# Moving fill work in a two-layer encoder trunk: the recurrence's evacuation, local attention, sample steps and embedding tiles

## The reference

```
h = x + 0.5 * RMSNorm(SwiGLU_1(RMSNorm(x)))
u = RMSNorm(h); [branch inputs | gate logits] = u @ w_in
four branches on u, each 256 wide:
  A conv module   B HGRN2 gated recurrence   C sliding-window attention   D stick-breaking attention
y_n = o_n @ w_branch[n];  m = sum_n sigmoid(gate_n) * y_n;  mix = m @ w_out
h = h + RMSNorm(mix);  h = h + 0.5 * RMSNorm(SwiGLU_2(RMSNorm(h)))
h = h + RMSNorm((p[i] @ ple_w) * sigmoid(RMSNorm(h) @ ple_gate_w))
```

## Time and profile before

| what | value |
|---|---|
| median of 3 runs | 3288.26 us (3283.48 to 3296.35) |
| profiled execution, its own time | 3279.91 us |
| its span, first to last instruction | 3278.2 us |
| PE busy | 3162.7 us, 96% of the span |
| mean granted clock of PE | 0.982 |
| ACT, DVE, POOL busy | 1079.8, 958.7, 1179.9 us |

### The profile page before, as it was taken

The page is one execution under the profiler, slowest core; times in us unless marked ns, Lnnn a source line. Parts: engine busy times, 40 slices in busy tenths (PEclk is TensorE's granted clock), DMA queues, the critical chain, the costliest instruction groups (busy, mean ns, idle before and its releaser), DMA issues.

```text
span 3278.2 us, 55957 instructions
## 1 busy us (share of the span) xinstructions
PE 3162.7 (96%) x24207; PEld 3049.5 (93%) x24207; DVE 958.7 (29%) x1417; ACT 1079.8 (33%) x1536; POOL 1179.9 (36%) x564
## 2 busy tenths in 40 slices
PE   8999999999999999999999999999999999999998
PEld 8999999996799999999999999989868999999988
DVE  3111024744443311101331110249334433111023
ACT  3233232235433332322433222322454333322222
POOL 6334333331234433333343433323212434333333
PEclk9999999999999999999899999999999999999988
DMA  3222222221122222322122222222211222222211
GB/s 102 83 80 78 83 63 66 78 71 41 45 78 83 58 83 78 88 83 68 58 63 79 83 80 82 65 56 85 62 41 53 82 78 58 83 83 88 81 52 62
DMA packets 455959, 236.31 MB, mean 72 GB/s; under 512 B 18630, under 2 KB 454150, under 8 KB 455814
## 3 DMA queue, kind: packets, MB, share of 16 engines
q1 hardware_dynamic: 445792, 227.05, 23.8%
q10 hardware_dynamic: 10022, 7.15, 0.7%
HBM read 228.53 MB, written 5.63 MB: 71 GB/s over the span
## 4 chain that ended last, share of the span: by engine, by line
PE 89%; DVE 5%; ACT 3%; POOL 1%; issue 1%; ACTq 1%; POOLq 0%; DVEq 0%
PE ps L594 79%; PE ps L626 3%; PE ps L634 1%; PE ps L1538 1%; PE ps L1848 1%; DVE uf L825 1%; PE ps L1556 1%; PE ps L1518 1%; DVE u_lo L819 1%; POOL u_lo L819 1%; ACT u_hi L743 0%; DVE kgate L1135 0%; PE ps L1542 0%; PE ps L1527 0%; DVE att L1153 0%
## 5 line engine op out<-in xcount | busy, mean ns | idle before, releaser
L1988 POOL TENSOR_TENSOR wlo<-wraw,whi 128x1024 fp32r<-128x1024 f32 (+1 forms) x432 | 1042.8, 2418 | 1934.9 <-ACT whi L556 1934.6
L594 PE MATMUL ps<-u_hi,whi 128*128 128x288 f32 x4800 | 1051.4, 300 | 37.5 <-ACT ybr L1714 11.8
L594 PE MATMUL ps<-u_lo,whi 128*128 128x288 f32 x4800 | 1033.8, 296 | 0.0
L594 PE MATMUL ps<-u_hi,wlo 128*128 128x288 f32 x4800 | 1033.3, 296 | 0.0
L594 PEld LDWEIGHTS ps<-u_hi,whi 128*128 128x128 f32 x4800 | 770.2, 189 | 72.6 <-issue 32.9
L594 PEld LDWEIGHTS ps<-u_hi,wlo 128*128 128x128 f32 x4800 | 774.1, 189 | 0.0
L594 PEld LDWEIGHTS ps<-u_lo,whi 128*128 128x128 f32 x4800 | 774.0, 189 | 0.0
L556 ACT ACTIVATE whi<-wraw 128x1024 fp32r<-128x1024 f32 (+1 forms) x432 | 449.3, 1040 | 559.3 <-PE ps L594 332.1
L868 DVE TENSOR_TENSOR sq<-sq,ps 128x576 f32<-128x576 f32 x88 | 66.3, 754 | 900.6 <-PE ps L594 900.6
L594 PE MATMUL ps<-s_hi,whi 128*128 128x288 f32 x1408 | 303.1, 296 | 0.0
L594 PE MATMUL ps<-s_hi,wlo 128*128 128x288 f32 x1408 | 302.7, 296 | 0.0
(11 more groups left out here) (268 smaller groups left out, 2595.5 us busy)
## 6 DMA issues: line engine op xcount, KB each, us to landing
wraw<-in_ffn_up SPq DMA_DIRECT2D x176, 512.0 KB, 3.8
wraw<-in_w_in SPq DMA_DIRECT2D x104, 512.0 KB, 3.8
wraw<-in_ffn_down SPq DMA_DIRECT2D x64, 512.0 KB, 3.7
wraw<-in_ffn_down SPq DMA_DIRECT2D x32, 384.0 KB, 3.4
wraw<-in_w_out SPq DMA_DIRECT2D x16, 512.0 KB, 3.8
wraw<-in_ple_gate_w SPq DMA_DIRECT2D x16, 512.0 KB, 3.8
wraw<-in_w_branch SPq DMA_DIRECT2D x16, 256.0 KB, 2.8
xtok<-in_x_prompt SPq DMA_DIRECT2D x4, 512.0 KB, 6.4
```

The source lines that it names most:

```text
L594: ins = pe.matmul(ps[:, 2 * p + f, 0:HT], wt[:, part, w], x[:, k, HT * f:HT * f + HT], start=start and n == 0 and c == 0, stop=stop and n ...
L1988: pool.tensor_tensor(wlo[:, i % SLOTS, 0:width(i)], wraw[:, i % SLOTS, 0:width(i)], whi[:, i % SLOTS, 0:width(i)], ALU.subtract).then_inc( ...
```

## The change

No product is added or removed. Five things move.

1. **Recurrence.** Two quarters of fill instead of one follow `hg_values` on TensorE, one fewer comes after the factors. On ScalarE, the evacuation and rounding of the unit that ends there, and the table load, go behind the copies and squares of the recurrence.
2. **Local attention.** Its three units of fill go in quarters instead of thirds: eleven steps instead of nine, and the twelfth quarter after the transposes of `pe_sb_tok`. Its evacuation stands behind the four cache stores.
3. **Sample steps.** The two gate-logit units of output tile 0 become kept gates 16 and 17, written to `sg`. `sb_fill` gives steps 16 to 21 two quarters each.
4. **Gates.** For m = 0, TensorE has only the branch unit; the sigmoids are taken from `sg` in place. The hardware loop is written out.
5. **Embedding.** Three tiles stand ahead of the square sums, two among them, one before the root, two after the factors; it was two, three, none and three.

```diff
-            gate_out: 2 * KD, gate_sig: 10,
+            gate_out: 2 * KD + 2, gate_sig: 10,
...
+            N_KEPT = 2 * KD + 2
+            BRANCHES = [U0_PAIR + 2] + [U0_PAIR + 3 * m for m in range(1, KD)]
...
@@ pe_hg, act_hg
                 hg_values(pe)
-                pe_fill(pe, 1)
+                pe_fill(pe, 2)
...
-                act_fill(act, 6)
+                act_fill(act, 5)
...
             def act_hg_norm(act):
-                act.preload_act_table_set(ROOT_SET)
                 for c in range(2):
                     act.wait_ge(hg_out, c + 1 + before(hg_out))
...
                     act.activation(sq[:, c, :], of[:, 2 + c, :], ACT.Square).then_inc(hg_sq, 1)
+                act.preload_act_table_set(ROOT_SET)
+                act_fill(act, 2)
...
-                act_fill(act, 4)
+                act_fill(act, 3)
...
@@ act_gate_part
-                    act.activation(halves(gkeep[:, g, :]), pair(0), ACT.Copy).then_inc(gate_out, 1)
+                    dst = gkeep[:, g, :] if g < 2 * KD else sg[:, g - 2 * KD, :]
+                    act.activation(halves(dst), pair(0), ACT.Copy).then_inc(gate_out, 1)
...
@@ pe_sw (act_sw alike)
-                    pe_gate_part(pe, GATES_CONV, GATES_SW, i, THIRDS)
+                    pe_gate_part(pe, GATES_CONV, GATES_SW, i, QUARTERS)
...
+            def sb_fill(i):
+
+                at = lambda j: min(max(j, 2 * j - 16), 4 * (N_KEPT - GATES_SW))
+                return range(at(i), at(i + 1))
...
@@ pe_sb (act_sb alike)
-                    pe_gate_part(pe, GATES_SW, 2 * KD, i, QUARTERS)
+                    for step in sb_fill(i):
+                        pe_gate_part(pe, GATES_SW, N_KEPT, step, QUARTERS)
...
@@ act_sb
                 out("sb_v_sample", 0, DEC, sbtok[0:64, 4, 256:512])
+
+                act_gate_part(act, GATES_CONV, GATES_SW, len(SW) + 2, QUARTERS)
...
@@ pe_gates
-                with pe.Fori(0, 2) as it:
-                    for m in range(4):
...
+                for m in range(KD):
+                    u0 = U0_PAIR + 3 * m
+                    split_ready(pe, BRANCHES[m])
+                    if m == 0:
+                        pe.wait_ge(gate_out, N_KEPT + before(gate_out))
...
+                    ins.then_inc(unit_done, 1)
+                    if m:
                         for n in (2, 3):
...
+                            products(pe, (u0 + n - 1) % SLOTS, u_hi, u_lo, range(KD), 0, n, True, True).then_inc(unit_done, 1)
 
-                        pe.wait_ge(yb_out, it * 16 + (4 * m + 4) + before(yb_out))
+                    pe.wait_ge(yb_out, 4 * m + 4 + before(yb_out))
...
@@ act_gates
-                        if n == 3:
+                        if n == 3 and m:
                             act_round(act, u0 + 2)
...
-                        act.wait_ge(unit_done, done(u0 + n - 1))
-                        act.activation(halves(sg[:, n - 2, :]), pair(n), ACT.Sigmoid).then_inc(sig_done, 1)
-                        act_round(act, u0 + n + 1)
+                        if m:
+                            act.wait_ge(unit_done, done(u0 + n - 1))
+                            act.activation(halves(sg[:, n - 2, :]), pair(n), ACT.Sigmoid).then_inc(sig_done, 1)
+                        else:
+                            act.wait_ge(gate_out, 2 * KD + n - 1 + before(gate_out))
+                            act.activation(sg[:, n - 2, :], sg[:, n - 2, :], ACT.Sigmoid).then_inc(sig_done, 1)
+                        if m or n == 3:
+                            act_round(act, u0 + n + 1)
...
@@ pe_mixer
                     hg_norm_factors(pe, c)
-                pe_fill(pe, 3)
+                pe_fill(pe, 2)
...
                 pe_sb_tok(pe)
+                pe_gate_part(pe, GATES_CONV, GATES_SW, len(SW) + 2, QUARTERS)
                 pe_sb(pe)
...
@@ pe_ple
-                e_tile(0)
-                e_tile(1)
+                for j in range(3):
+                    e_tile(j)
                 for k in range(KD):
                     h_sums(pe, N_PPRE, k)
-                    if k in (1, 3, 5):
-                        e_tile(2 + k // 2)
+                    if k in (1, 3):
+                        e_tile(3 + k // 2)
+                e_tile(5)
...
-                for j in range(5, KD):
-                    e_tile(j)
+                e_tile(6)
+                e_tile(7)
...
@@ act_ple
                 act_root(act, N_PPRE)
+                e_tile(5)
                 for k in range(KD):
                     u_high_tile(act, N_PPRE, k)
-                    if k in (1, 3, 5):
+                    if k in (2, 4):
                         e_tile(5 + k // 2)
```

More of the change, by code:

```diff
@@ L541, in crow @@
                 return rows_all[:, at:at + 1]
+            N_KEPT = 2 * KD + 2
+            BRANCHES = [U0_PAIR + 2] + [U0_PAIR + 3 * m for m in range(1, KD)]
             def dmas(i):
                 i = i % UNITS
-                return 4 if U0_PAIR <= i < U0_OUT and (i - U0_PAIR) % 3 == 0 else 2 if i - U0_PROJ in (SQ_, SQ_ + 1) else 1
+                return 4 if i in BRANCHES else 2 if i - U0_PROJ in (SQ_, SQ_ + 1) else 1
             def landed(i):
@@ L1440, in act_sw @@
                         act.activation(of[:, 4:6, 64 * (i - 2):64 * (i - 2) + 64], ps[:, 2 + i % 2, 0:128].rearrange("p (g q) -> p g q", g=2), ACT.Copy).then_inc(sw_o, 1)
-                    act_gate_part(act, GATES_CONV, GATES_SW, i, THIRDS)
+                    act_gate_part(act, GATES_CONV, GATES_SW, i, QUARTERS)
             def dve_sw(dve):
@@ L1621, in act_sb @@
                         evac(i - 2)
-                    act_gate_part(act, GATES_SW, 2 * KD, i, QUARTERS)
+                    for step in sb_fill(i):
+                        act_gate_part(act, GATES_SW, N_KEPT, step, QUARTERS)
             def dve_sb(dve):
@@ L1672, in pe_gates @@
             def pe_gates(pe):
-                with pe.Fori(0, 2) as it:
-                    for m in range(4):
-                        u0 = U0_PAIR + 3 * m
-                        i = it * 12 + u0
-                        split_ready(pe, i)
-                        if m == 0:
-                            pe.wait_ge(gate_out, 2 * KD + before(gate_out))
-                        for n in range(NB):
-                            if m == 0:
-                                pe.wait_ge(o_ready, 2 * n + 2 + before(o_ready))
-                            if n >= 2:
-                                pe.wait_ge(sig_done, it * 8 + (2 * m + n - 1) + before(sig_done))
-                            ins = products(pe, u0 % SLOTS, o_hi, o_lo, (2 * n, 2 * n + 1), 2 * n, n, True, True)
-                        ins.then_inc(unit_done, 1)
+                for m in range(KD):
[3 more added lines that the diff above has]
+                        pe.wait_ge(gate_out, N_KEPT + before(gate_out))
+                    for n in range(NB):
+                        if m == 0:
+                            pe.wait_ge(o_ready, 2 * n + 2 + before(o_ready))
+                        if n >= 2:
+                            pe.wait_ge(sig_done, 2 * m + n - 1 + before(sig_done))
+                        ins = products(pe, BRANCHES[m] % SLOTS, o_hi, o_lo, (2 * n, 2 * n + 1), 2 * n, n, True, True)
+                    ins.then_inc(unit_done, 1)
+                    if m:
                         for n in (2, 3):
-                            split_ready(pe, i + (n - 1))
-                            pe.wait_ge(yb_out, it * 16 + (4 * m + n - 1) + before(yb_out))
+                            split_ready(pe, u0 + n - 1)
+                            pe.wait_ge(yb_out, 4 * m + n - 1 + before(yb_out))
                             products(pe, (u0 + n - 1) % SLOTS, u_hi, u_lo, range(KD), 0, n, True, True).then_inc(unit_done, 1)
-                        pe.wait_ge(yb_out, it * 16 + (4 * m + 4) + before(yb_out))
+                    pe.wait_ge(yb_out, 4 * m + 4 + before(yb_out))
             def pe_out(pe):
@@ L1709, in act_gates @@
                     u0 = U0_PAIR + 3 * m
-                    act.wait_ge(unit_done, done(u0))
+                    act.wait_ge(unit_done, done(BRANCHES[m]))
                     if m:
@@ L1958, in layer_sync, with load_gates @@
                 for m in range(KD):
-                    i = U0_PAIR + 3 * m
+                    def load_gates():
+                        for n in (2, 3):
+                            cg = C_GATE + D * n + 128 * m
+                            i = U0_PAIR + 3 * m + n - (1 if m else 2)
+                            load_unit(sp_, i % SLOTS, i, cols(a["w_in"], L, slice(cg, cg + 128)))
+                    if m == 0:
+                        load_gates()
+                    i = BRANCHES[m]
                     slot, c = i % SLOTS, slice(128 * m, 128 * m + 128)
@@ L1968, in layer_sync @@
                     sp_.dma_start(v[:, 6:8, :], cols(wb, L, c, 6, 2)).then_inc(w_loaded[slot], 16)
-                    for n in (2, 3):
-                        cg = C_GATE + D * n + 128 * m
```

(3 more changed lines are left out.)

## The result

The changed kernel takes 3260.9 us (median of 16 runs, 3246.7 to 3277.2), the kernel before 3287.7 us in the same runs. The ratio is 0.992 (95% interval 0.9903 to 0.9936): faster by 27 us (21 to 32), inside the forecast's range, with a gain of 27 where 39.5 was forecast. The profiled execution took 3254.2 us, 25.7 less than that of before.

The account below looks back on a forecast made before the run. TensorE, busy 3162.7 of 3278.2 us, bounds the kernel; only idle time and half clock can move. Two layers: 18 + 27 - 4 - 1.5 = 39.5 us off 3288.3 gives 3249 us (chance 0.76), range 3234 to 3272.

Parts of the forecast that it names:

- 12.6 us from 579.55: Recurrence: time from the fill's end to the convolution's transposes, against 21.9 us before; a gain of 9.2 us a layer.
- half of 3.65: Recurrence: the two factor products at full clock, put at 1.83 us by halving a row taken as half clock.
- The price of the table loads: Recurrence: each load on ScalarE ahead of the root costs its row of 1.28 us, with no added drain.
- Forecast 13.5 us: Embedding stage: the factors end 13.5 us a layer earlier; with later losses, a gain of 10 to 13.6.
- the 3.7 forecast: Embedding stage, behind the factors: waits grow to about 3.7 us in small pieces, as one tile less covers them.
- I charge 2 us a layer, from 0 to 4: Local attention: loss per layer from the late evacuation and rounding, the mask and some shift.
- The argument that waits of 1.27 us stand at full clock: Against the clock staying low: waits of 1.27 and 1.31 us already stood in stretches at full clock.
- I charge 0.7 us a layer: Sample steps and start of the gates: waits and half clock, from a gain of 0.5 to a loss of 2.4.
- Attention falls behind: Rival, local attention: all nine steps wait for VectorE and the split, 6 us more lost a layer; 3261 us, chance 0.05.
- Clock not given back: Rival, recurrence and embedding: waits go but small ones keep the clock low; gain 16 us, 3272 us, chance 0.10.
- Table switches: Rival, recurrence: loads cost more than their rows, root 4.1 us later; gain 24 us, 3264 us, chance 0.05.
- The slower rival: Gates: low clock runs on through three branches in each layer, costing 117 us; 3366 us, chance 0.04.

Follow-up runs that it names:

- one_load: Kernel before with only the recurrence and embedding parts of the change, without the early load of the root's table: 3235.9 us against 3286.8, ratio 0.9852.
- early_evac: The change, but in local attention ScalarE copies the finished unit out ahead of the step's exponentials, rounding left in place: 3245.6 us against 3283.4, ratio 0.9904.
- cover_moved: The change with late rounding, no early table load, pairwise second branch release, early copy, twelfth quarter as fill in stick-breaking's first step: 3242.2 us, ratio 0.9878.

## Why the prediction was right or wrong

**Recurrence: right in mechanism, 1.2 us short.** The forecast counts 12.6 us from 579.55, the end of the first quarter, so 14.2 from the first fill product; measured 15.38. The gain is 8.4 and 7.7 us, for 9.2. The waits came where they were forecast: 1.35 at the factors for 1.0, 0.72 ahead of the transposes for 0.8. The term that was mis-sized besides is the factors, "half of 3.65": that row had run only in part at half clock, and at full clock the products take 2.25 us (594.47 to 596.72) for the 1.83 forecast. The price of the table loads was read rightly from its row: each of the three takes 1.28 us, and the next instruction starts 0.01 us later. By the drain of the Trainium skill's page ScalarE: Activation LUTs (section What ACT_TABLE_LOAD costs) the wait at the factors would have been an estimated 5 us. It was 1.35 us, and no such gap stands between the rows shown at one_load.

**Embedding: right.** Forecast 13.5 us, measured 13.8, a little over the upper end of 13.6. The waits behind the factors came as small pieces, 2.2 us in sum for the 3.7 forecast, the longest 1.00 us, and kept the clock.

**Local attention: wrong in size.** The failing step is "I charge 2 us a layer, from 0 to 4"; measured 5.6 (6.7 and 3.9 against the profiled execution of before alone, which had a longer wait there in layer 1). The 2 us held idle time only: the evacuation behind the stores (seen, 1.78 us of wait) and some shift. Two things were missed. The wait of 1.27 us in the steps didn't just move, it grew to 2.28. With quarters it was 2.05 to 2.28 in all eight layers traced without an early copy; with thirds it was 1.17 to 1.35 in eight of twelve and 2.01 to 2.51 in the other four, all in layer 1. That less cover per step brings TensorE to it earlier fits, but what lengthens it in those four is open. And behind both waits the clock fell (0.76 and 0.72 in the windows above), which cost more than the waits did. The stage of layer 0 in windows, before and then after the change (columns as above):

```profile
720.98:784.58 63.60, 58.51 (x429) 48.15 (x429) 31.13 (x91) 32.16 (x92) 7.57 (x4) 0.97 0.16 48
```

```profile
718.99:789.33 70.34, 63.67 (x429) 51.34 (x429) 32.31 (x91) 32.29 (x92) 7.55 (x4) 0.90 0.15 44
```

The same 429 products keep TensorE busy for 5.2 us longer, at a mean clock of 0.90 for 0.97, and its idle time grows by only 1.6 us. The argument that waits of 1.27 us stand at full clock was true of rows, but the new waits were no longer of that size.

**Sample steps and gates: wrong in size.** The failing step is "I charge 0.7 us a layer", with 2.4 as its end; measured 2.8. The mechanisms were all there: 5.11 us for the outputs' low part, forecast 4.5; 2.37 behind the first branch product, forecast 2.4. Half clock took 2.4 us of the first branch product (8.9 us for a unit of 6.5) and 1.6 of the second: 4.0, where 1.6 to 4.5 were allowed and 2.8 is what the charge holds. And each of the seven later waits for branch copies grew from 0.74 to 0.83, 0.6 us that no term held.

**The sum.** With the measured terms a layer gains 8.0 + 13.8 - 5.6 - 2.8 = 13.4, two layers 27; the times say 27 (21 to 32). That they meet so closely is in part luck, since attention scatters by 2 us and more. Of the 12.7 us between forecast and result attention holds 7 (2 x 3.6), the gates 4 (2 x 2.1) and the recurrence 2 (2 x 1.2), less 0.6 won in the embedding stage. The range's ends don't follow from its own terms: gains of 47 and 15 with 5 us of spread give 3236 to 3278, not 3234 to 3272. The result lies inside either.

**The rivals.** "Attention falls behind" (3261) had the place and the sign: a layer lost 3.6 us more than charged, for the 6 it named, though not step by step but at two waits and their half clock. That its time was met is luck, since the gates and the recurrence made up the difference. "Clock not given back" was wrong where it was put, in the recurrence and the embedding stage. "Table switches" fell. The slower rival didn't come: full clock was back by 898.

## What to carry to other kernels

A wait that is made shorter pays twice, and so does a wait that a moved piece of work creates: price it with the half clock that follows at its new length, not at its old one. Cover taken from a step in which two engines are near balance came back as idle time here, wherever the copies were put (early_evac, cover_moved). A stage length compares two kernels only when its two landmarks enclose the same work in both. And an edit of several parts is worth taking apart: two of these four gave 45 us, all four 27, and three of them, without the quarters in attention and with small repairs, 60.

## What the runs showed of the hardware

**How long a wait was, and the clock behind it.** In ten profiled executions (all kernels here but early_evac and cover_moved) the granted clock over the 6 us behind TensorE's waits, called low under 0.85, reads: after waits for a unit's copy in local attention of 1.17 to 1.35 us, full in 8 of 8; of 1.77 to 2.51 us, low in 16 of 18; after the 2.28 us ahead of the scores, low in 18 of 20; after 2.70 to 5.11 us ahead of the first branch product, low in 20 of 20. In early_evac and cover_moved, waits of 1.13 to 1.55 us for the scores' probabilities left it full in 8 of 8.

**A coin toss in the norms.** One wait was different: 1.18 us ahead of a norm's square sums, much the same in every kernel and five of the 13 of the earlier trace rows. In twelve profiled executions it was followed by half clock in 10 of 58 cases. In the profiled execution of the change:

```profile
461.88 16.14 PE L630 MATMUL ps<-ones,sq 128*128 128x64 f32 x80 [1.18 <-ACT sq L726]
...
483.43 0.50 PE L598 MATMUL ps<-u_hi,whi 128*128 128x288 f32 x2 [1.11 <-DVE u_lo L823]
```

The 80 products took 16.1 us, where the kernel before took 9.45, and the first unit behind came 21.6 us after their start, where it came 14.0: one such case costs 7.6 us. There are five such norms in a run, so two or three more or fewer would make up much of the spread of the runs (3246 to 3277); that they do was not tried. What decides the toss stays open. One toss alone is worth 7 us of a single time; the stage lengths above leave these norms out.
